# A trunk step whose first stage moves to token rows, with unread matmuls at the even attention's entry and w_mod in 512-column transfers

## The reference

```python
def rmsnorm(x, g):
    xf = x.astype(jnp.float32)
    y = xf * lax.rsqrt(jnp.mean(xf * xf, axis=-1, keepdims=True) + EPS)
    return (y * g.astype(jnp.float32)).astype(x.dtype)

def trunk_layer(l, x, cvec, prm, ctx):
    mod = jax.nn.silu(cvec) @ prm["w_mod"][l] + prm["b_mod"][l]
    shift1, scale1, gate1, shift2, scale2, gate2 = jnp.split(mod, N_MOD, axis=-1)
    h = rmsnorm(x, prm["norm_pre"][l, 0]) * (1.0 + scale1) + shift1
    ...
        mix, new_ctx = even_mixer(h, ...)
    ...
    x = x + gate1 * rmsnorm(mix, prm["norm_post"][l, 0])
    h = rmsnorm(x, prm["norm_pre"][l, 1]) * (1.0 + scale2) + shift2
    f = conv_ffn(h, ...)
    x = x + gate2 * rmsnorm(f, prm["norm_post"][l, 1])
```

## Time and profile before

| | us |
|---|---|
| median of 3 runs | 1928.89 (1928.62 to 1929.17) |
| the profiled execution, its own time | 1928.23 |
| its span | 1926.4 |
| PE busy | 1841.1 |
| DVE busy | 963.8 |
| ACT busy | 827.9 |

### The profile page before, as it was taken

One profiled execution on the slowest core, in us unless ns is written; L12 is line 12 of the kernel. 1 busy time (PEld: TensorE's weight loads), 2 busy tenths in 40 slices (PEclk: granted clock), 3 DMA queues, 4 the chain that ended last, 5 costly groups with the idle time before them and its releaser, 6 DMA issues.

```text
span 1926.4 us, 36263 instructions
## 1 busy us (share of the span) xinstructions
PE 1841.1 (96%) x14824; PEld 1698.8 (88%) x14824; DVE 963.8 (50%) x1613; ACT 827.9 (43%) x1420; POOL 55.0 (3%) x76
## 2 busy tenths in 40 slices
PE   6999998888899999999999999999999999999998
PEld 3999966667799999999999887776899999999997
DVE  4433355556746655235555743344375553255555
ACT  4545422225745544124445653343464441244453
POOL 0000122220000000000000000000000000000000
PEclk9999999998999999999999999999999999999999
DMA  7222366531021223222234311110211232122243
GB/s 284 65 58 66 128 252 221 199 141 51 1 71 44 77 71 87 71 66 68 73 94 140 95 44 32 27 35 28 67 44 55 76 87 78 55 76 76 78 136 115
DMA packets 238723, 170.23 MB, mean 88 GB/s; under 512 B 20139, under 2 KB 230285, under 8 KB 232333
## 3 DMA queue, kind: packets, MB, share of 16 engines
q1 hardware_dynamic: 238604, 168.54, 28.2%
HBM read 165.08 MB, written 3.44 MB: 87 GB/s over the span
## 4 chain that ended last, share of the span: by engine, by line
PE 85%; DVE 6%; ACT 4%; issue 3%; DMA 1%; SPq 0%; ACTq 0%; DVEq 0%
PE ps L2007 46%; PE ps L2083 15%; PE ps L2040 4%; PE ps L2201 3%; PE ps L2708 2%; PE ps L2745 2%; PE ps L2704 2%; PE ps L2398 1%; PE ps L2220 1%; PE ps L2578 1%; PE ps L2451 1%; PE ps L2555 1%; PE ps L2211 1%; PE ps L2028 1%; ACT w_hi L782 1%
## 5 line engine op out<-in xcount | busy, mean ns | idle before, releaser
L782 ACT ACTIVATE w_hi<-w_raw 128x1024 fp32r<-128x1024 f32 (+4 forms) x187 | 198.6, 1062 | 559.6 <-PE ps L2007 436.0
L1366 DVE TENSOR_TENSOR w_lo<-w_raw,w_hi 128x1024 fp32r<-128x1024 f32 (+4 forms) x191 | 234.2, 1227 | 377.2 <-ACT w_hi L782 376.8
L2007 PE MATMUL ps<-h_hi,w_hi 128*128 128x322 f32 x1648 | 381.5, 313 | 3.2 <-ACT conv L972 1.7
L2007 PE MATMUL ps<-h_lo,w_hi 128*128 128x322 f32 x1648 | 380.2, 312 | 0.0
L2007 PE MATMUL ps<-h_hi,w_lo 128*128 128x322 f32 x1648 | 378.1, 310 | 0.0
L2007 PEld LDWEIGHTS ps<-h_hi,w_hi 128*128 128x128 f32 x1648 | 278.1, 189 | 4.8 <-ACT conv L1192 2.0
L2007 PEld LDWEIGHTS ps<-h_hi,w_lo 128*128 128x128 f32 x1648 | 279.1, 189 | 0.0
L2007 PEld LDWEIGHTS ps<-h_lo,w_hi 128*128 128x128 f32 x1648 | 279.1, 189 | 0.0
L2083 PE MATMUL ps<-g_hi,w_hi 128*128 128x322 f32 x352 | 110.7, 314 | 2.7 <-DVE g_lo L1850 1.6
L2083 PE MATMUL ps<-g_lo,w_hi 128*128 128x322 f32 x352 | 109.6, 311 | 0.0
L2083 PE MATMUL ps<-g_hi,w_lo 128*128 128x322 f32 x352 | 109.1, 310 | 0.0
...
## 6 DMA issues: line engine op xcount, KB each, us to landing
...
```

The lines of the kernel that those rows point to most:

```text
L782: act.activation(WH[slot][:, 0:k, :], RAW[slot][:, 0:k, :], ACT.Copy).then_inc(w_hi, 1)
L1366: dve.tensor_tensor(WL[slot][:, 0:k, :], RAW[slot][:, 0:k, :], WH[slot][:, 0:k, :].bitcast(F32), ALU.subtract).then_inc(w_lo, 1)
L2007: last = pe.matmul(out, w_of(k, wi), x_of(k, xi, i), start=(k == 0 and p == 0), stop=(k == ks - 1 and p == 2))
```

## The change

Three parts.

1. The first stage works on token rows. ACT issues the x tiles itself, and behind them the first two blocks of ev_w_in, ahead of w_mod. The sum of squares of each token is taken along its row, three tiles by ACT and two by DVE; the rows are scaled into `x_unit_rows` (three by DVE, two by ACT), and PE turns these and the unscaled rows: ten tiles of 8 transposes instead of five, in two pairs of banks. The first six parts of w_mod lie between them, and the weight splits of the first two blocks between the copies. Gain and shift go straight into `h_hi` (ACT), while DVE makes the same affine product once more into `x_affine` and subtracts. The eight sums of squares over chunks, the matmul over partitions, the inverse root of 644 columns, the four wide products and the eight copies are gone. `keep_busy` shrinks from 3 and 12 matmuls to 1, 1 and 5.
2. At the even attention's entry PE waits for DVE's last rotation (`a_rotated`), issues 3 unread matmuls, and only then waits for the DeltaNet's last output; 4 more stand behind the first scores. They write bank 7.
3. Each of the 40 w_mod blocks of the DeltaNet stage is sent as four transfers of 512 columns; the wait counts 64 instead of 16.

The diff, cut to its core:

```diff
-    NORMS = (("first", KD, 1), ("l2", 8, 8), ("on", 4, 8), ("cq", C_Q // P, 1), ("ckv", C_KV // P, 1))
+    BY_ACT, BY_DVE, W_AT = (0, 1, 2), (3, 4), (5, 7)
+    NORMS = (("first", 0, 0), ("l2", 8, 8), ("on", 4, 8), ("cq", C_Q // P, 1), ("ckv", C_KV // P, 1))
...
+    XS = [place(f"x_unit_rows{t}", [D], R_W + D * t) for t in range(NT)]
+    XNA = [place(f"x_affine{s}", [TW], R_A + al(TW) * s) for s in range(2)]
+    XSUM = place("x_row_sum", [8], R_SC)
+    XRST = place("x_row_rstd", [8], R_SC + 8)
...
             rows(VR[3], 8, a["b_mod"].rearrange("l (m p) -> (l m) p", p=P))
-            for t in range(NT):
-                src = a["x_prompt"][0] if t == 0 else a["x_sample"][0, (t - 1) * P:t * P, :]
-                sp.dma_start(XR[t][:, :], src).then_inc(S("x_landed"), 16)
             wm = [a["w_mod"][l].rearrange("(k p) m -> p k m", p=P) for l in range(2)]
             for k in range(KD):
                 sp.dma_start(MWS[k][:, :], wm[0][:, k, 0:2 * D]).then_inc(S(f"mod_landed{k}"), 16)
-            for n in range(23):
+            for n in range(2, 23):
...
                 if u >= MSLOTS:
                     sp.wait_ge(S("mod_done"), KD + u - MSLOTS + 1)
                 l, m0 = mod_columns_of(u // KD)
-                sp.dma_start(MW[u % MSLOTS][:, :], wm[l][:, u % KD, m0:m0 + 2 * D]).then_inc(S(f"mod_landed{u % MSLOTS}"), 16)
+                for j in range(4):
+                    sp.dma_start(MW[u % MSLOTS][:, 512 * j:512 * j + 512], wm[l][:, u % KD, m0 + 512 * j:m0 + 512 * j + 512]
+                                 ).then_inc(S(f"mod_landed{u % MSLOTS}"), 16)
             for u in range(MSLOTS):
...
             pool.memset(EPSC[:, :], EPS).then_inc(S("gpsimd_filled"), 1)
-            pool.wait_ge(S("rows_turned"), 2 * NT)
             pool.wait_ge(S("mod_done"), KD)
+            zero_gaps(S("gpsimd_filled"), *H2)
+            pool.wait_ge(S("rows_turned"), RT0)
             pool.memset(QKV[:, :, 0:1], 0.0)
             pool.memset(QKV[:, :, TW - 1:TW], 0.0).then_inc(S("gpsimd_filled"), 1)
...
                 for k in range(KD):
                     h_chunk(i, k)
+            for t in range(NT):
+                src = a["x_prompt"][0] if t == 0 else a["x_sample"][0, (t - 1) * P:t * P, :]
+                act.dma_start(XR[t][:, :], src).then_inc(S("x_landed"), 16)
+            for n in range(2):
+                act.dma_start(RAW[n][:, 0:KD, :], ein_v[:, :, (6 + n) * P:(7 + n) * P]).then_inc(w_landed[n], 16)
             act.preload_act_table_set("natural_log_exp_and_others")
-            act.wait_ge(S("vec_cols"), 2)
+            act.wait_ge(S("x_landed"), 16 * NT)
+            for t in BY_ACT:
+                act.activation(XS[t][:, :], XR[t][:, :], ACT.Square, accum_out=XSUM[:, t:t + 1]).then_inc(S("norm_sq"), 1)
+            act.wait_ge(*filled("eps"))
+            act.wait_ge(S("norm_sq"), len(BY_ACT))
+            act.wait_ge(S("norm_sum"), len(BY_DVE))
+            act.activation(XRST[:, 0:NT], XSUM[:, 0:NT], ACT.Ln, scale=1.0 / D, bias=EPSC[:, 0:1]).then_inc(S("norm_ln"), 1)
+            act.wait_ge(S("norm_ln"), 1)
+            act.activation(XRST[:, 0:NT], XRST[:, 0:NT], ACT.Exp, scale=-0.5).then_inc(S("norm_rstd"), 1)
+            act.wait_ge(S("vec_cols"), 1)
             act.activation(SCE[:, :], VC[:, 0:16], ACT.Exp, scale=-1.0).then_inc(S("exp_c"), 1)
-
-            for t in range(NT):
-                act.wait_ge(S("rows_turned"), 2 * t + 1)
-                act.activation(X[:, 0:4, TILES[t]:TILES[t] + P], bank(6).rearrange("p (k c) -> p k c", c=P),
+            act.wait_ge(S("norm_rstd"), 1)
+            for t in BY_DVE:
+                act.activation(XS[t][:, :], XR[t][:, :], ACT.Copy, scale=XRST[:, t:t + 1]).then_inc(S("h_shifted"), 1)
+            for y in range(2 * NT):
+                dst, t = ((XN, X)[y // NT], y % NT)
+                act.wait_ge(S("rows_turned"), 2 * y + 1)
+                act.activation(dst[:, 0:4, TILES[t]:TILES[t] + P], bank((6, 2)[y % 2]).rearrange("p (k c) -> p k c", c=P),
                                ACT.Copy).then_inc(S("rows_copied_a"), 1)
+                if y in W_AT:
+                    hi(W_AT.index(y))
+            act.wait_ge(S("mod_ready"), 1)
+            act.wait_ge(*filled("h_gaps"))
             act.wait_ge(S("rows_copied_a"), NT)
             act.wait_ge(S("rows_copied_v"), NT)
-            act.wait_ge(*filled("eps"))
-            squares("first", lambda k: X[:, k, :], lambda k: None, KD)
-            rstd("first", D)
-            hi(0)
-            hi(1)
-            act.wait_ge(S("mod_ready"), 1)
             for k in range(KD):
-                act.wait_ge(S("h_scaled"), k // 2 + 1)
                 for c, c0, c1 in CONDS:
-                    last = act.activation(XN[:, k, c0:c1], XN[:, k, c0:c1], ACT.Identity, bias=MOD[0][:, 2 * k + c:2 * k + c + 1],
+                    last = act.activation(Hh[:, k, c0:c1], XN[:, k, c0:c1], ACT.Identity, bias=MOD[0][:, 2 * k + c:2 * k + c + 1],
                                           scale=PA[0][0][:, 2 * k + c:2 * k + c + 1])
-                last.then_inc(S("h_shifted"), 1)
-                act.wait_ge(S("h_shifted"), k + 1)
-                act.activation(Hh[:, k, :], XN[:, k, :], ACT.Copy).then_inc(S("h_hi"), 1)
+                last.then_inc(S("h_hi"), 1)
             RL = [ACC, RST]
...
             dve.memset(X[:, :, 0:1], 0.0)
             dve.memset(X[:, :, P0 + PROMPT:S0], 0.0)
             dve.memset(X[:, :, S0 + SAMPLE:TW], 0.0)
+            dve.wait_ge(S("x_landed"), 16 * NT)
+            for t in BY_DVE:
+                dve.tensor_tensor_reduce(XS[t][:, :], XR[t][:, :], XR[t][:, :], 1.0, 0.0, ALU.mult, ALU.add, XSUM[:, t:t + 1]
+                                         ).then_inc(S("norm_sum"), 1)
             dve.wait_ge(S("vec_turned"), 4)
             dve.tensor_copy(VC[:, 0:122], bank(4, 122)).then_inc(S("vec_cols"), 1)
             dve.tensor_copy(VC[:, 128:488], PS[:, 4 * 512 + 128:4 * 512 + 488]).then_inc(S("vec_cols"), 1)
+            step(dve.memset(SCX[:, :, :], 0.0))
+            dve.wait_ge(S("norm_rstd"), 1)
+            for t in BY_ACT:
+                dve.tensor_scalar(XS[t][:, :], XR[t][:, :], XRST[:, t:t + 1], None, ALU.mult).then_inc(S("h_scaled"), 1)
             dve.wait_ge(S("exp_c"), 1)
             step(dve.tensor_scalar(SCR[:, :], SCE[:, :], 1.0, None, ALU.add))
             step(dve.reciprocal(SCR[:, :], SCR[:, :]))
-            step(dve.memset(SCX[:, :, :], 0.0))
             dve.tensor_tensor(SCX[:, :, 0:2], SCR[:, :].rearrange("p (q k) -> p k q", q=2),
                               VC[:, 0:16].rearrange("p (q k) -> p k q", q=2), ALU.mult).then_inc(S("silu_c"), 1)
-            for t in range(NT):
-                dve.wait_ge(S("rows_turned"), 2 * t + 2)
-                dve.tensor_copy(X[:, 4:8, TILES[t]:TILES[t] + P], q4(bank(7))).then_inc(S("rows_copied_v"), 1)
-            dve.wait_ge(*filled("eps"))
-            sums("first", KD)
-            dve.wait_ge(*of("rstd", "first", 1))
-
-            def x_unit(j):
-
-                dve.tensor_tensor(XN[:, 2 * j:2 * j + 2, :], X[:, 2 * j:2 * j + 2, :],
-                                  RST[:, :].unsqueeze(1).broadcast_to([P, 2, TW]), ALU.mult).then_inc(S("h_scaled"), 1)
-            x_unit(0)
-            x_unit(1)
+            for y in range(2 * NT):
+                dst, t = ((XN, X)[y // NT], y % NT)
+                dve.wait_ge(S("rows_turned"), 2 * y + 2)
+                dve.tensor_copy(dst[:, 4:8, TILES[t]:TILES[t] + P], q4(bank((7, 3)[y % 2]))).then_inc(S("rows_copied_v"), 1)
+                if y in W_AT:
+                    w_rest(W_AT.index(y))
             dve.wait_ge(S("mod_done"), KD)
             dve.tensor_copy(MROW0[:, :], bank(0)).then_inc(S("mod_rows"), 1)
-            x_unit(2)
             dve.wait_ge(S("mod_turned"), 1)
             mod_columns(0, 0, 5, "mod_cols")
             gains(0, 0, 1, "mod_ready")
-            w_rest(0)
-            x_unit(3)
-            w_rest(1)
+            dve.wait_ge(S("rows_copied_a"), NT)
+            dve.wait_ge(S("rows_copied_v"), NT)
             for k in range(KD):
+                if k >= 2:
+                    dve.wait_ge(S("h_lo"), k - 1)
+                for c, c0, c1 in CONDS:
+                    q = 2 * k + c
+                    step(dve.tensor_scalar(XNA[k % 2][:, c0:c1], XN[:, k, c0:c1], PA[0][0][:, q:q + 1], MOD[0][:, q:q + 1],
+                                           ALU.mult, ALU.add)) if c else dve.tensor_scalar(
+                        XNA[k % 2][:, c0:c1], XN[:, k, c0:c1], PA[0][0][:, q:q + 1], MOD[0][:, q:q + 1], ALU.mult, ALU.add)
                 dve.wait_ge(S("h_hi"), k + 1)
-                dve.tensor_tensor(Hl[:, k, :], XN[:, k, :], Hh[:, k, :].bitcast(F32), ALU.subtract).then_inc(S("h_lo"), 1)
+                dve.tensor_tensor(Hl[:, k, :], XNA[k % 2][:, :], Hh[:, k, :].bitcast(F32), ALU.subtract).then_inc(S("h_lo"), 1)
...
             pe.wait_ge(S("vec_landed"), 16 * 12)
```

(49 more changed lines are left out.)

37 lines of the change are left out of this document (21 added, 16 removed).

## The result

The change makes the kernel slower: 1938.17 us, median of 13 runs (1933.9 to 1944.0), against 1929.17 (13 runs, 1926.9 to 1939.2) of the kernel before on the same chips; ratio 1.0044, 95% interval 1.0031 to 1.0057. The forecast was 1914.6. Single runs spread more than the three shown ahead of the prediction, by some 10 us in either kernel. The profiled execution of the changed kernel took 1940.4 us, its span is 1938.6.

The account below looks back on a forecast made before the run. PE, busy 1841 of 1926 us, was taken as the bound; gains of 4.5 + 4.3 + 5.5 = 14.3 us off 1928.2 gave 1913.9, and the median's 0.66 above that 1914.6 us; range 1908 to 1924.

Parts of the forecast that it names:

- more starved fetches: Rival, DeltaNet stage: four times as many transfers ahead of a fetch, 31 waits of 1.23 us; 1949.6 us; chance 0.05.
- slow quarters: Rival, DeltaNet stage: w_mod in quarters gives nothing back and costs 3.9 us; 1924.0 us; chance 0.06.
- The chain on rows: First stage: from x's landing at 10.5 us, squares, root and scaling make the rows ready at 17.2 us.
- the rival by the rule of the Trainium skill: Rival, first stage: transposes don't raise PE's clock, 52 of them at 0.217 cost 5.6 us; 1920.2 us; chance 0.04.
- the clock falls all the same: Rival, even attention's entry: PE's clock still drops to half despite the fillers, 4.6 us; 1919.2 us; chance 0.08.
- The price of a fall: Even attention's entry: time lost when the clock drops to half, 3.9 us in three pairs plus 0.7 before them.

Follow-up runs that it names:

- e1_whole: The changed kernel with each w_mod block sent again in one transfer of 1 MB; 1930.3 us, ratio 0.9996 against the kernel before.
- e3_first_only: The changed kernel with w_mod in transfers of 1 MB and without the seven unread matmuls at the attention's entry; 1931.7 us, ratio 1.0017 against the kernel before.

## Why the prediction was wrong

**Part 3, w_mod in quarters: a gain of 5.5 us forecast, a loss of 6 to 9 measured. This is the step that failed.** The prediction said: "With packets a quarter as long the wait should fall", and took three quarters of the waits, "the share by which a packet shrinks". The reading ahead of it was right: they are waits for instructions, and they need w_mod's traffic. But nothing in the rows said that a fetch waits for one packet, and it does not: quarters made the waits longer (13 to 15 us for 9), and slow transfers made them four times as long. The fetch's own packet took no longer in quarters; it began later. The waits grow with the time for which w_mod keeps the DMA full, 3.06 us for 1 MB in quarters and not 2.88. Whether these 6% are the whole cause, or four transfers in the queue for one have a part, stays open. The range of this part, 0 to 8.6, had its lower end wrong; nothing in the trace excluded a loss. A second thing was not in the sum at all: what a wait of 2 us costs when the clock falls behind it. The rival "more starved fetches" named the right wait and the right direction, and had 0.05; that it is the number of transfers which does it, as that rival has it, is not shown. Its price was off (29.5 us for 31 waits of 1.23), since not every fetch starves: 11 or 12 do, for 1.1 to 1.4 us in the mean.

The rule of the Trainium skill, DMA: Bandwidth & Descriptors, section "Bandwidth", which asks for transfers of 1 MiB or more, was right in its direction. With quarters of 256 KB the engines needed 6% more time for 1 MB, with many transfers under way; yet the loss was not, as the rival "slow quarters" had it, in waits for w_mod (0.8 us more), but in PE's instructions.

**Part 1, the first stage: 4.5 forecast, 3.3 in this trace**, and 2.4 us between the means of ten traces (42.3 to 43.5) and of five of the old form (44.3 to 45.9), leaving out two at 46 and those with the late split; with the two it is 1.9. The chain on rows came within 0.1 us, by two errors that cancel: x landed at 11.0 for 10.5, and the chain took 6.2 us for 6.7. The clock rose in the transposes as forecast: the first 32 took 6.43 us, eight later ones 1.09, and the weight loads fell from 231 ns to 141 among the first 32, with nothing between them. So the rival by the rule of the Trainium skill, TensorE: Matmul & The Clock Gate, section "Part 4: PE-mode transpose", is out. Of the 1.3 us that are missing against 41.3, 0.9 is PE's own pace: 80 transposes took 12.8 us for 11.8, since at full clock one takes 0.129 us (eight take up 1.03) and not 0.109, so w_mod was done at 38.1. The other 0.4 is DVE, which came late to the row sums: the splits were costed at nothing, with their cover named, but the second block landed at 35 us, since transfers of 512-byte runs share the engines with 8 MB of w_mod. When it lands at 37.7, the same order costs 3.4 us.

**Part 2, the attention's entry: 4.3 forecast, about none measured** (1.4 between e1_whole and e3_first_only, within their spread). The bounds had held it (-0.3 to 4.6), and the rival "the clock falls all the same" had 0.08. The price of a fall was nearly right: 4.2 us, from 86.7 to 90.9, for 4.6. What the prediction missed is that the fall in the one trace of the kernel before was not the rule: of five traces without fillers three have none. Nor do seven fillers hold the clock: of twelve traces with them six fell, later. The gain was computed against an execution with bad luck.

**The range.** It was put together from one execution and from three times within 0.6 us. Thirteen runs spread over 12 us.
